# Two sequence-mixing blocks in one kernel: block products made in passes, the scan's gate projected earlier, other planner tables

## The reference

```python
for l in range(2):
    x = x + 0.5 * swiglu(rms_norm(x, ffn1_norm[l]), ffn1_w_gate[l], ffn1_w_up[l], ffn1_w_down[l])
    u = rms_norm(x, mix_norm[l]) @ w_in[l]
    z, xbc, dt_raw, q_lat, kv_lat, k_pe, c_h, c_b, c_c = split(u)
    y_ssd = ssd_mixer(z, xbc, dt_raw, ...)       # conv of xbc, silu; two-way scan; y * silu(z); group norm
    y_mla = mla_mixer(q_lat, kv_lat, k_pe, ...)  # attention from latent q, k, v; norm
    y_conv = group_rms_norm(c_b * depthwise_conv(c_c * c_h, conv_w), ...)
    x = x + concatenate([y_ssd, y_mla, y_conv]) @ w_out[l]
    x = x + 0.5 * swiglu(rms_norm(x, ffn2_norm[l]), ffn2_w_gate[l], ffn2_w_up[l], ffn2_w_down[l])
for l in range(2):
    x = hybrid_layer(x, ...)   # differential attention and an mLSTM, gated, projected by w_o
```

## Time and profile before

| | |
|---|---|
| median of three runs | 1864.54 us |
| profiled execution | 1864.64 us, of which span 1862.8 us |
| TensorE busy | 1847.7 us, 99% |
| VectorE busy | 1216.8 us, 65% |
| ScalarE busy | 1057.0 us, 57% |
| GpSimd busy | 107.2 us, 6% |
| matmuls | 9674 |
| from HBM | 307.16 MB, 165 GB/s over the span |

### The profile page before, as it was taken

One profiled execution on the slowest core, in us unless ns is written; L12 is line 12 of the kernel. 1 busy time (PEld: TensorE's weight loads), 2 busy tenths in 40 slices (PEclk: granted clock), 3 DMA queues, 4 the chain that ended last, 5 costly groups with the idle time before them and its releaser, 6 DMA issues.

```text
span 1862.8 us, 24631 instructions
## 1 busy us (share of the span) xinstructions
PE 1847.7 (99%) x9674; PEld 1562.2 (84%) x9674; DVE 1216.8 (65%) x1872; ACT 1057.0 (57%) x1557; POOL 107.2 (6%) x85
## 2 busy tenths in 40 slices
PE   9999999999999999999999999999999999999999
PEld 7888998788888888899888888888878888888887
DVE  5654787865555555578876555587757478775845
ACT  5444677555444444476756444566776456667742
POOL 0000110000000000011000000001101000110100
PEclk9999999999999999999999999999999999999999
DMA  7555553335555555553334555554445555544553
GB/s 289 183 189 178 163 170 103 114 128 189 181 186 187 188 185 183 184 166 135 114 105 156 183 188 185 171 183 155 138 150 172 187 169 182 160 135 146 171 191 115
DMA packets 86579, 309.82 MB, mean 166 GB/s; under 512 B 9648, under 2 KB 10288, under 8 KB 86464
## 3 DMA queue, kind: packets, MB, share of 16 engines
q1 hardware_dynamic: 85680, 306.35, 49.4%
q0 software_dynamic: 496, 1.65, 0.2%
q10 hardware_dynamic: 288, 0.25, 0.0%
HBM read 307.16 MB, written 1.05 MB: 165 GB/s over the span
## 4 chain that ended last, share of the span: by engine, by line
PE 88%; DVE 6%; ACT 4%; issue 1%; POOL 1%; DVEq 0%; ACTq 0%
PE bank L1120 84%; PE bank L1117 4%; DVE WL L1970 2%; DVE XC L2120 1%; ACT WH L1518 1%; ACT PA L1518 1%; POOL STATS L2717 1%; ACT L1518 1%; ACT MP L1518 1%; DVE PA L2587 0%; DVE BO L2569 0%; DVE BO L2577 0%; ACT XC L1518 0%; DVE XBG L2097 0%; DVE STATS L2285 0%
## 5 line engine op out<-in xcount | busy, mean ns | idle before, releaser
L1970 DVE TENSOR_TENSOR WL<-RAW,WH 128x1024 fp32r<-128x1024 f32 x585 | 705.7, 1212 | 444.6 <-ACT WH L1518 439.9
L1518 ACT ACTIVATE WH<-RAW 128x1024 fp32r<-128x1024 f32 (+2 forms) x587 | 609.6, 1048 | 462.1 <-PE bank L1120 459.7
L1120 PE MATMUL bank<-WH,XTH 128*128 128x512 f32 (+1 forms) x1376 | 544.3, 396 | 0.5 <-DVE WL L1965 0.5
L1120 PE MATMUL bank<-WL,XTH 128*128 128x512 f32 (+1 forms) x1376 | 535.5, 389 | 0.0
L1120 PE MATMUL bank<-WH,XTL 128*128 128x512 f32 (+1 forms) x1376 | 535.2, 389 | 0.0
L1120 PE MATMUL bank<-WH,FR 128*128 128x512 f32 x1264 | 391.9, 391 | 0.0
L1120 PEld LDWEIGHTS bank<-WH,XTH 128*128 128x128 f32 x1376 | 258.5, 188 | 55.0 <-issue 3.4
L1120 PEld LDWEIGHTS bank<-WL,XTH 128*128 128x128 f32 x1376 | 258.3, 188 | 53.5
L1120 PEld LDWEIGHTS bank<-WH,XTL 128*128 128x128 f32 x1376 | 258.6, 188 | 51.8 <-issue 1.4
L1120 PEld LDWEIGHTS bank<-WH,FR 128*128 128x128 f32 x1264 | 234.0, 188 | 47.4
L1120 PE MATMUL bank<-WL,FR 128*128 128x512 f32 x632 | 247.1, 391 | 0.0
(11 more groups left out here) (317 smaller groups left out, 1626.3 us busy)
## 6 DMA issues: line engine op xcount, KB each, us to landing
RAW<-in_WALL_dram SPq DMA_DIRECT2D x569, 512.0 KB, 3.3
RAW<-in_WALL_dram SPq DMA_DIRECT2D x8, 448.0 KB, 3.3
RAW<-in_WALL_dram SPq DMA_DIRECT2D x8, 256.0 KB, 2.6
X<-in_x_dram SPq DMA_DIRECT2D x4, 256.0 KB, 5.1
out_dram<-X SPq DMA_DIRECT2D x4, 256.0 KB, 2.0
ROWP<-in_ROWP_dram POOLq DMA_DIRECT2D x1, 672.0 KB, 10.2
CONSTS<-in_CST_dram POOLq DMA_DIRECT2D x1, 664.0 KB, 7.8
ROUNDED<-in_CSTR_dram POOLq DMA_DIRECT2D x1, 208.0 KB, 12.9
```

What stands on the lines that cost most here:

```text
L1120: return self.e.matmul(out, lhs, rhs, start=start, stop=stop, skip_group_check=True)
L1518: return self.e.activation(out, in_, func, **k)
L1970: self.e.tensor_tensor(lo, raw, hi.bitcast(F32), ALU.subtract).then_inc(*self.up("lo", j))
```

## The change

- The three terms of a block are made in passes: the first term for all chunks and halves of the block (of one half in the last block of a projection), then the second, then the third. The block waits for `hi` at its begin, for `left_hi` of a chunk ahead of its first term, for `left` ahead of the second, for `lo` ahead of the third.
- The first block of the kernel makes the first and second term chunk by chunk as its high parts come, then the third term of both chunks.
- `late_x` comes behind block 1, with `split 2` ahead of its flips.
- In the mixers z's two halves are projected behind xbc, ahead of ch, pr and yc.
- `Order.start` lets a block start up to a third of a pass earlier against its left chunks and its low weights (`hi_ends`, `halves`, `length` are new).
- The tables `WORK`, `HOP`, `LEAD` and `RULE` have other numbers; the mixers' `LEAD` has two more entries. `WORK` is shown cut.

```diff
 WORK = {
-    "xsq": "A160", "rstd": "V41 G176", "rows_x": "V61", "rows": "P18 A80", "lat_sq": "A99", "lat_var": "V24 G121",
+    "xsq": "A160", "rstd": "V45 G193", "rows_x": "V61", "rows": "P14 A80", "lat_sq": "A99", "lat_var": "V24 G121",
...
-HOP = {"P": 15, "A": 6, "V": 11, "G": 45}
+HOP = {"P": 25, "A": 6, "V": 1, "G": 80}
...
-        "sums": 40, "flips": 80, "evicted": 180, "steps": -20,
+        "sums": -180, "flips": 20, "evicted": 50, "steps": 180,
...
-        "qk": 70, "mla_head": 330, "rope1": -50, "decay": -50, "states": 100, "segment": -20, "finish": 60, "flips": -90,
-        "conv": 100, "conv2": -140, "evicted": 60, "sums": 30, "kpe": -300, "skip": -200, "heads": 100, "lat": 20,
+        "qk": 230, "mla_head": 360, "rope1": -50, "decay": -20, "states": 140, "segment": 30, "finish": -100, "flips": 300,
+        "conv": 100, "conv2": 60, "evicted": 300, "sums": -100, "kpe": 30, "skip": -20, "heads": 250, "lat": 20, "cn": -10,
+        "rows": 150,
...
-        "hq": -100, "diff_head": 30, "sums": 30, "chain": 30, "hb_t": -200, "u": -250, "rows": 140, "hb": -100, "pair": 300,
-        "hconv": -10, "bz": 300, "evicted": 340, "flips": -130, "steps": 250, "oan": 110,
+        "hq": -270, "diff_head": 140, "sums": 60, "chain": -50, "hb_t": -130, "u": -30, "rows": 180, "hb": 200, "pair": 300,
+        "hconv": 180, "bz": 30, "evicted": 340, "steps": 30, "oan": 20,
...
-RULE = {"ffn": (0, 20, 40), "mix": (420, 120, 80), "hyb": (560, 60, 0)}
+RULE = {"ffn": (60, 240, 40), "mix": (420, 100, 80), "hyb": (500, 0, 20)}
...
     def late_x(self):
 
+        self.add("split", 2)
         for c in (4, 6):
             self.add("flip", "x", 0, c, 2)
-            self.add("split", c // 2)
+        self.add("split", 3)
...
     def start(self, lin):
 
         n, when = len(lin.blocks), self.at["P"]
+        third = self.length(lin, n) // (6 if n == len(lin.parts) - 1 else 3)
         for c in lin.parts[n]:
             phase = self.left(*lin.src, c)
             if phase not in self.ends:
                 return NEVER
-            when = max(when, self.ends[phase])
+            when = max(when, self.halves[phase], self.ends[phase] - third)
...
-        return max(when, self.split_ends.get(len(self.blocks), NEVER))
+        j = len(self.blocks)
+        return max(when, self.hi_ends.get(j, NEVER), self.split_ends.get(j, NEVER) - 2 * third)
...
-        if j == 0:
+        if j == 1:
             self.late_x()
...
+        self.run([lin("z", 0, 512, "tok", (0,))])
+        self.run([lin("z", 512, 512, "tok", (1,))])
         self.run([lin("ch", 3008, 512, "feat")])
         self.run([lin("pr", 4032, 512, "feat", after=[("evict", ("ch", i))])])
         self.run([lin("yc", 3520, 512, "feat", after=[("conv2", i, 3)])])
-        self.run([lin("z", 0, 512, "tok", (0,))])
-        self.run([lin("z", 512, 512, "tok", (1,))])
...
+        w.wait_ge(*self.at("hi", j))
+        whole = last and lin.kind != "thin"
+        for halves in ((0,), (1,)) if whole else ((0,),) if lin.kind == "thin" else ((0, 1),):
+            for x in passes:
+                if x == 2:
+                    w.wait_ge(*self.at("lo", j))
+                for n, c in chunks:
+                    if x == 0:
+                        self.left_hi_made(lin.src, c)
+                    elif x == 1:
+                        self.left_made(lin.src, c)
+                    for half in halves:
+                        m = self.products(lin, half, x, xh[:, c, :], xl[:, c, :], hi[:, n, :], lo[:, n, :], first and n == 0,
+                                          last and n == len(kk) - 1)
+            if whole and halves == (0,):
+                m.then_inc(*self.up("half", lin.key))
+        m.then_inc(*self.up("block", j))
...
+        left, right = (xl if x == 1 else xh), (lo if x == 2 else hi)
+        st, en = st and x == 0, en and x == 2
```

More of the change, by code:

```diff
@@ L251, in __init__ @@
         self.ends, self.split_ends, self.owed, self.table = {}, {j: 0 for j in range(NSPLIT)}, [], None
+        self.hi_ends, self.halves = {j: 0 for j in range(NSPLIT)}, {}
         self.small, self.taken, self.empty = (6, 7), 0, {}
@@ L289, in add @@
                 first = since
+            if step[0] == "A":
+                self.halves[phase] = since
         for b in self.next_small(name):
@@ L360, in split @@
         self.at["A"] = max(self.at["A"], free) + 20 + 86 * size // 1024
+        self.hi_ends[j] = self.at["A"] + HOP["A"]
         self.at["V"] = max(self.at["V"], self.at["A"] + HOP["A"]) + 20 + 102 * size // 1024
@@ L426, in start, with length @@
             when = max(when, min(self.freed.get(p, 0) for p in free))
-        return max(when, self.split_ends.get(len(self.blocks), NEVER))
+        j = len(self.blocks)
+        return max(when, self.hi_ends.get(j, NEVER), self.split_ends.get(j, NEVER) - 2 * third)
+    def length(self, lin, n):
+        return max((272 if lin.kind == "tok" else 288) * len(lin.parts[n]) * lin.w // 1024, 60)
     def block(self, lin, when):
@@ L440, in block @@
         self.phases.append(("block", j))
-        self.at["P"] = when + max((272 if lin.kind == "tok" else 288) * size // 1024, 60)
+        self.at["P"] = when + self.length(lin, n)
         self.ends["block", j] = self.at["P"] + HOP["P"]
-        if j == 0:
+        if j == 1:
             self.late_x()
@@ L1141, in block @@
         xh, xl = k.left(lin.src[0])
[L1142 to L1157, removed]
-            m.then_inc(*self.up("block", j))
+        chunks = list(enumerate(kk))
@@ new lines, in block @@
+        passes = (0, 1, 2)
+        if j == 0:
+            self.left_hi_made(lin.src, kk[0])
+            for n, c in chunks:
+                w.wait_ge(*(self.at("hi", 0) if n else self.at("hi_first", 0)))
+                for x in (0, 1):
+                    if x:
+                        self.left_made(lin.src, c)
+                    for half in range(2):
+                        self.products(lin, half, x, xh[:, c, :], xl[:, c, :], hi[:, n, :], lo[:, n, :], first and n == 0, False)
+            for n, c in chunks:
+                w.wait_ge(*(self.at("lo", 0) if n else self.at("lo_first", 0)))
+                for half in range(2):
+                    m = self.products(lin, half, 2, xh[:, c, :], xl[:, c, :], hi[:, n, :], lo[:, n, :], False, False)
+            m.then_inc(*self.up("block", j))
+            return
@@ L1162, in block, with left_hi_made @@
                 self.emptied[lin.pair[t]] = (by, (lin.key, t))
+    def left_hi_made(self, src, c):
+        name = src[0]
+        if name == "y" and c >= 12:
+            self.w.wait_ge(*self.at("cn_act", (src[1], "hi", c - 12)))
+            return
+        if name == "y":
+            name = "ys" if c < 8 else "mo"
+        self.w.wait_ge(*self.at("left_hi", (name, src[1], c // 2 * 2)))
     def left_made(self, src, c):
@@ L1169, in left_made, with products @@
         self.w.wait_ge(*self.at("left", (name, src[1], c)))
-    def products(self, lin, half, xh, xl, hi, lo, st, en):
+    def products(self, lin, half, x, xh, xl, hi, lo, st, en):
         ps = self.k.PS[lin.pair[half]]
+        left, right = (xl if x == 1 else xh), (lo if x == 2 else hi)
+        st, en = st and x == 0, en and x == 2
         if st:
@@ L1176, in products @@
         if lin.kind == "tok":
-            o, s = ps[:, 0:lin.w], slice(128 * half, 128 * half + 128)
-            self.mm(o, xh[:, s], hi, st, False)
-            self.mm(o, xl[:, s], hi, False, False)
-            return self.mm(o, xh[:, s], lo, False, en)
+            return self.mm(ps[:, 0:lin.w], left[:, 128 * half:128 * half + 128], right, st, en)
         if lin.kind == "thin":
-            o = ps[0:16, 0:256]
-            self.mm(o, hi, xh, st, False)
-            self.mm(o, hi, xl, False, False)
-            return self.mm(o, lo, xh, False, en)
+            return self.mm(ps[0:16, 0:256], right, left, st, en)
         for f in range(2):
-            o, fs = ps[:, 256 * f:256 * f + 256], slice(256 * half + 128 * f, 256 * half + 128 * f + 128)
-            self.mm(o, hi[:, fs], xh, st and f == 0, False)
-            self.mm(o, hi[:, fs], xl, False, False)
-            m = self.mm(o, lo[:, fs], xh, False, en)
+            fs = slice(256 * half + 128 * f, 256 * half + 128 * f + 128)
+            m = self.mm(ps[:, 256 * f:256 * f + 256], right[:, fs], left, st and f == 0, en)
         return m
```

## The result

The changed kernel takes 1875.55 us (median of three runs, 1874.15 to 1877.29) against 1864.54: a ratio of 1.0059 with a 95% interval of 1.0045 to 1.0073. It is 11.0 us slower. The forecast was 1859.0 with a range of 1851 to 1868, so both the sign and the range were wrong.

The account below looks back on a forecast made before the run. TensorE's queue length plus its holes was taken to bound the kernel. Passes 0, start -0.2, gate projection -3.6 and tables -1.8 summed to -5.6 us: 1864.6 to 1859.0, range 1851 to 1868.

Parts of the forecast that it names:

- The gate projection first, -3.6: Two mixers: z ahead of the convolution branch frees VectorE for the scan; 4.6 us gained, less 0.5 a mixer for new waits.
- If the scan starts some 3 us earlier, both go: Mixers: TensorE's holes at the silu before x's transposes and at the scan's end vanish, 2.3 us a mixer.
- the prediction's own rule: TensorE's waits: each costs its shown idle time plus some 0.16 us that the modelled matmul ends cover.
- My limits of this term: Mixers, z first: -6.6 us if attention's probability waits go too, +6 if no wait goes and the convolution branch comes late.
- the eight matmuls of the scan's tail: End of the scan: they take 1.5 us where four take 0.36, priced as 0.7 us more.
- The tables, -1.8: Small groups between blocks: half of 3.6 us of waits in two hybrid layers goes, nothing in feed-forward; between -3.6 and +2.
- Other leads either take these groups apart or don't: Hybrid layers: reason for taking half of the two waits' 3.6 us, -1.8 us.
- The passes, 0: All blocks: the new term order leaves the pace at 2.72 and 2.75 us; it could have been +10 or -5 us.
- The start, -0.2: Kernel start: first block at about 8.27 gains 0.54, but block 2 waits for x's late flips until 15.2; 0.2 us remains.
- Slower: Rival, 0.17: convolution branch too late for the output projection, 3 us a mixer, 1870; or slower pace of passes, 1874.
- The time of 1870: Mixers: time of the late convolution branch rival, 1864.6 + 6 - 0.2, with z first's gains gone.
- The rule of the Trainium skill: ScalarE in attention: z's silu adds two table switches a mixer, 5.3 us by the page, 2.6 by the rows; not reaching TensorE.

Follow-up runs that it names:

- e4: Changed kernel with z projected last again, behind yc; passes and new tables stay: 1862.91 us, ratio 0.9991.
- e7: Kernel before with the new tables and z first, but terms made chunk by chunk, no passes: 1878.39 us, ratio 1.0075.
- e11: e4 with only z's first 512 columns projected ahead of ch, pr and yc, the second 512 last: 1874.24 us, ratio 1.0053.
- e6: Changed kernel plus 20 unread constant matmuls ahead of the first wout block of the scan's columns in each mixer: 1872.90 us, ratio 1.0044.
- e5: Changed kernel with the squaring of the scan's last quarter put behind the copies of the first scan flips: 1869.49 us, ratio 1.0026.
- e1: Kernel before with the new tables alone (z last, three terms together): 1865.50 us, ratio 1.0005.
- e10: e4 with the old tables and old rule of start from the first hybrid layer on: 1860.91 us, ratio 0.9980.
- e8: Changed kernel with the old tables (passes and z first stay): 1904.88 us, ratio 1.022.
- e9: Kernel before with only the terms made in passes; old tables, z last, old start rule and flips' place, same phase order: 1863.52 us, ratio 0.9993.
- e3: Changed kernel with old tables and z last; passes, new rule of start and later x flips stay: 1874.26 us, ratio 1.0052.
- e12: e10 with the flips of x's chunks 4 to 7 set back behind the first block: 1859.81 us, ratio 0.9975.
- e2: Kernel before with z projected ahead of ch, pr and yc alone (old tables, three terms together): 1899.35 us, ratio 1.0186.

## Why the prediction was wrong

*The gate projection first, -3.6: the failing step.* I wrote "If the scan starts some 3 us earlier, both go". The scan did not start earlier but 4 us later, 4.9 counted from the mixer's start. I had reasoned from VectorE's load in a wide window, as if work taken out of a queue let everything behind it move up. But the instruction order is written by the planner, and with other blocks it wrote another: the silu of the scan's x stands four blocks behind attention's last product, in e4 one. And the end of the scan, where I had seen only 1.8 us to win, is the most delicate place: a chain of VectorE and ScalarE (product, squaring, norm, flips, copies) with only a few blocks to cover it. In the three orders that the planner wrote for z or half of it first under the new tables (the change, e7, e11), one of its links came out 1.9 to 3.4 us late in both mixers. In place of -3.6 stands +12.6 (the change against e4).

Where the 12.6 us lie is read from the length of a mixer: 223.3 us in the change, 221.7 with the idle filled (e6), 220.1 with the flip copies ahead (e5), 216.9 with z last (e4). So of 6.4 us a mixer 1.6 are the low clock and 1.6 the longer wait, both shown by an edit; by the medians the two together are 6.1 us of the kernel. The other 3.2 a mixer (6.6 us for both by the medians) are left in e5. Idle time shown grows there by 1.9 us a mixer against e4, nearly all of it in seven places where e4 has no wait: 0.71 for the silu before the scan's transposes, 0.61 that is left of the wait for the flips' copies, 0.25 before the scan's first product, 0.12 in attention and three under 0.1. With the 0.16 us that each wait hides, by the prediction's own rule, they come to 3.0 of the 3.2. That an earlier scan would remove them is not shown: no run moved the scan's inputs forward by themselves.

*My limits of this term* (-6.6 to +6) held no price for a mere reordering inside ScalarE's queue, and none for the clock. I had noted that the granted clock was 1.00 in each stretch, and left out what it would do behind a longer idle. A smaller slip: the eight matmuls of the scan's tail cost 1.51 - 0.72 = 0.8 us more than eight would elsewhere, not 0.7.

*The tables, -1.8.* The sign was wrong in the hybrid layers (+2.4 instead, shown by e1 and undone by e10) and the mixers, which I had not priced, gained 1.5 in the two (e1). "Other leads either take these groups apart or don't" treated the tables as an edit by itself. The larger fact is that they belong to the order: without them the two other parts cost 40 us (e8).

*The passes, 0.* The pace was right: 2.72 us for a block before and after, and e9 shows no cost in 1863.52. What I never priced is the changed rule of `start`, some +10 us under the old tables. It lets a block stand directly behind the flips that it needs: in e3 the block on chunks 4 and 5 of the second hybrid layer comes directly behind their flips at 1536.62 and waits, and in the order before another block stands between. Under the new tables this loss isn't there: passes and rule together take 2.6 us off (e4 against e1) and 2.8 (the change against e7). They are no part of why the change is slower.

*The start, -0.2.* It brought 0.9 us to the first mixer, and some of that is luck of the one execution. The first block came at 7.40, not 8.27, since the transposes ahead of it came 0.75 us earlier (6.92 against 7.67), and the third at 14.55, not 15.2. But these transposes move from one execution to the next: they begin at 7.84 in e1 and 7.21 in e7, both with the old start. There the third block hardly follows them (15.36 and 15.25). With the new start it does: it comes at 15.27 in e8 and 15.31 in e11, where they begin at 7.74 and 7.79. So for transposes as late as in the kernel before, the forecast of 15.2 and -0.2 was right. The wait for the flips' copies that I had foreseen is there, 0.58 us, and e12 removes it.

*The rivals.* "Slower" had 0.17, and its mechanism was another: the output projection never waits for the convolution branch. Its wait is for the scan's flips, behind all four blocks of that branch. The time of 1870 was too low because the low clock and the late scan were not in it.

*The rule of the Trainium skill.* z's silu does bring table loads into attention: the change has 47 in all and e4, with z last, 43, so two more in each mixer, as foreseen. ScalarE there, changed kernel:

```profile
289.58 1.28 ACT L1550 ACT_TABLE_LOAD   x1
290.87 1.27 ACT L1550 ACTIVATE ZS<-bank,SUMS 128x512 f32<-128x512 f32 x2
292.16 1.28 ACT L1550 ACT_TABLE_LOAD   x1
293.45 0.57 ACT L1550 ACTIVATE MP<-bank,STATS 128x256 f32<-128x256 f32 x1
```

Each load takes 1.28 us and the activation behind it starts 1.29 us after the load began, against 1.30 in the earlier trace rows. The Trainium skill, "ScalarE: Activation LUTs", section "What ACT_TABLE_LOAD costs", adds a drain of some 1380 ns; this trace shows none at either load.

## What to carry to other kernels

Where a planner writes the order of in-order queues, a moved projection is not priced by the load that it shifts: look at the chain with the least cover (here the end of the scan) and ask which instruction might come to stand ahead of the one that TensorE needs next. A new rule for when work may start and the tables tuned for it are one edit: measure the combinations, and where a table helps one kind of stage and harms another, use it in the first only. Price a longer idle of TensorE at more than its length: here the low clock behind one of 2.5 us cost 1.6 us more.

## What the runs showed of the hardware

The granted clock fell to 0.5 for 3.4 us at each of the two idles of 2.52 us in the changed kernel, 0.4 and 0.7 us behind their ends. It did so behind the one of 2.41 us (with 0.63 more) in the passes alone, and behind the second but not the first of two equal idles of 1.91 and 0.58 us in e11; why only there is open. In e7, with two idles of 3.44 us, it fell 0.4 us behind the end of the first and 0.2 before the end of the second. In the four idles of 8.3 us (e2, e8) it fell while TensorE still stood, 1.7 to 4.6 us after the idle began, and the low stretch of 20.5 us ended 13.9 to 16.8 us behind the idle's end. Behind the waits of 1.13 us in the hybrid layers it never fell. Twenty matmuls of 256 columns that nobody reads, in the place of each 2.5 us idle, kept it at 1.0 and made the kernel 2.65 us faster.
